# Bidirectional RWKV beside neighbourhood attention: one scan for the decays, division at the attention's output, tails first in a round, both directions' sigmoids together

## The chip, the cores and the metric

One Trainium2 chip, one of its cores. The metric is the device time of one execution in microseconds, median of several runs.

## What is computed

A token sequence of 512 with 1024 channels goes through a first block of two layers (mixer, cross attention, convolutional FFN) and then a second block: RWKV7 in both directions, neighbourhood attention, sigmoid gates, an output projection and 32 routed experts. The change touches RWKV and attention, which in the reference read

```python
def rwkv_log_decay(lora, w0, up):
    w_raw = (w0 + jnp.tanh(lora) @ up).astype(jnp.float32)
    return -jnp.exp(-jax.nn.softplus(-w_raw) - 0.5)
def rwkv_step(S, inp):
    r_t, w_t, k_t, v_t, kk_t, a_t = inp
    sa = jnp.einsum('dbhij,dbhj->dbhi', S, -kk_t)
    S = (S * w_t[..., None, :] + sa[..., :, None] * (kk_t * a_t)[..., None, :]
         + v_t[..., :, None] * k_t[..., None, :])
    y = jnp.einsum('dbhij,dbhj->dbhi', S, r_t)
    return S, y
...
        s = jnp.where(col_mask[:, None, :], s, NEG_INF)
        prob = jax.nn.softmax(s, axis=(-2, -1))
        return jnp.einsum('bhqrk,bhrkd->bhqd', prob, v_blk)
```

The log of a decay is thus −e^−0.5 times a sigmoid. There are 8 RWKV heads of 64 channels and 8 attention heads of 64; the attention's window is 8 rows of 16 columns of a 64-column grid, and all 512 keys are scored with a bias that masks the rest.

## The kernel before

Everything is float32. Large projections stream their weights in units of 128x2048 numbers; ACT makes a high part (L552, `act_split`), DVE the low part (L556, `dve_split`), and PE multiplies three times (L569). Seven PSUM banks rotate: `take_bank` (L513) makes PE wait until the last reader of that bank has marked it. All waits are semaphore waits in an engine's own in-order queue.

RWKV is computed by **quarters** t = 0 to 3, each of 128 channels (two heads), in both directions d = 0, 1, over 8 chunks of 64 tokens. Each engine has a generator for each part: `quarter(t)` holds a key part (L2280, L2543, L2710) and two `direction(t, d)` parts (PE L2298, ACT L2556, DVE L2722, POOL L2913). A direction runs as follows.

- Preparation, PREP_STEPS = 8 steps: PE multiplies the low-rank inputs for decay and `a` (tile `rw_lora_w`; d picks the row half), ACT takes sigmoids (L2566, L2568), DVE scales the first by −e^−0.5 (`ts`, L596), scans it per chunk with a reset mask (L2737), and forms `before` = cumulative − own (L2747) and `rest` = total − cumulative (L2754; L2756 and L2757 for d = 1). ACT takes exponentials of these (DC, R, A, B at L2581–L2584, H at L2586), DVE multiplies them onto r, kk, k (L2750, L2762, L593, L2767, L2768), POOL multiplies H onto K and B for the token side (L2930, L2932).
- 22 steps: PE forms the chunks' products, a triangular inverse in six levels (products of `rw_X`, `rw_XT`, `rw_U`; ACT copies U at L2610; DVE masked copies L2800, L2803), the UW products (`rw_GA,rw_XT`, ACT copy L2626), four banks of MN products (`rw_TB,rw_UW`; DVE L2812, L2814, L2817) and seven steps of the state, each a PE product `rw_S,rw_MT` and a DVE add L2831.
- `tail(t)`, 5 steps: normalisation of y, bonus and gate.

**Attention** has 8 units u (four head pairs, two halves of the queries). A unit has four score tiles of 128x512: PE scores, DVE adds the bias and takes the maximum (L2880), ACT exponentiates with row sums (L2671), DVE takes the reciprocal of the sum (L2889) and multiplies the whole tile by it (L596), PE transposes sixteen 128x128 pieces (L2506), ACT copies them (L2680), PE multiplies with v, ACT copies the output 128x256 (L2688).

What orders all this is `side_by_side` (L2032): in each round every engine advances the running quarters' parts (key, d = 0, d = 1), then the tails, then, in four of five rounds, attention. A new quarter begins every NEXT_AT = 16 rounds, so its preparation lies beside the last rounds of the quarter before; the first one's lies beside the gate projections (`beside_gate`, L2028). All engines walk through the same rounds. SP issues the stores of finished parts (`y_spill`) and loads of weight units in the same order of rounds.

## Time and profile before

| | us |
|---|---|
| median of three runs (lowest, highest) | 2575.53 (2573.32, 2575.6) |
| profiled execution, its span | 2572.24, 2570.9 |
| PE busy | 2450.4 |
| DVE busy | 1390.5 |
| ACT busy | 943.4 |
| POOL busy | 244.0 |
| granted clock, mean over the span | 0.984 |

The profiled execution is a single one; its parts are read as times from the span's start. Busy times of different engines overlap. The granted clock is a share of TensorE's full speed.

### The profile page before, as it was taken

The page shows a single profiled execution, that of the slowest core. Times are in us where ns is not written, and L with a number is a line of the kernel's source. Part 1 is how long each engine was busy: PE and PEld are TensorE (multiplying, and loading weights), DVE is VectorE, ACT ScalarE, POOL GpSimd, SP SyncE. Part 2 cuts the span into 40 slices and gives each one's busy share as a digit, 9 for nine tenths or more (in the row PEclk, how much of TensorE's full clock was granted, in tenths as well). Part 3 has the DMA queues.
Part 4 walks back from the last instruction along what each step waited for, and adds up shares of the span by engine and source line. Part 5 has one row for each costly group of instructions (what it writes and reads, how often), then busy time and mean ns, then how long its engine had stood idle before and what let it go on. Part 6 is the DMA issues. An engine that isn't in the chain of part 4 may idle for free.

```text
span 2570.9 us, 40805 instructions
## 1 busy us (share of the span) xinstructions
PE 2450.4 (95%) x17416; PEld 1842.1 (72%) x17416; DVE 1390.5 (54%) x1951; ACT 943.4 (37%) x1276; POOL 244.0 (9%) x204
## 2 busy tenths in 40 slices
PE   8998999999999989999999999999888889899996
PEld 6777878888887658878888887877776677633332
DVE  6776446454556866446454557574567755511112
ACT  4454333232333244233232344334646643411111
POOL 1002010000000101010000020000011102133331
PEclk9999999999999999999999999999999999999998
DMA  4223222222223423222222224433312123499994
GB/s 184 88 77 120 102 82 99 98 93 104 83 99 117 141 89 115 99 82 99 98 96 100 83 98 151 176 123 128 82 34 44 40 97 131 186 373 380 380 398 169
DMA packets 100562, 343.18 MB, mean 133 GB/s; under 512 B 41376, under 2 KB 49952, under 8 KB 66592
## 3 DMA queue, kind: packets, MB, share of 16 engines
q1 hardware_dynamic: 86560, 332.15, 35.8%
q0 software_dynamic: 13824, 8.44, 1.1%
q8 instruction: 139, 2.28, 0.4%
q14 instruction: 39, 0.32, 0.0%
HBM read 368.31 MB, written 30.93 MB: 155 GB/s over the span
## 4 chain that ended last, share of the span: by engine, by line
PE 83%; DVE 8%; ACT 4%; DMA 2%; issue 2%; SPq 1%; POOL 0%; DVEq 0%; ACTq 0%; POOLq 0%
PE bank L569 81%; DVE w_lo L556 1%; PE bank L3178 1%; ACT w_hi L552 1%; DMA w_raw<-stream 1%; DVE square L1975 1%; ACT rw_LT L2600 0%; PE bank L2506 0%; DMA e_w_raw<-y_rows 0%; PE bank L3200 0%; SPq L1581 0%; DVE na_score L2880 0%; DMA x<-x_spill 0%; DMA xa_mem<-mem_in 0%; PE bank L2375 0%
## 5 line engine op out<-in xcount | busy, mean ns | idle before, releaser
L569 PE MATMUL bank<-xg_hi,w_hi 128*128 128x512 f32 x1568 | 618.5, 398 | 11.9 <-DVE xg_lo L593 11.9
L569 PE MATMUL bank<-xg_hi,w_lo 128*128 128x512 f32 x1536 | 598.8, 390 | 0.0
L569 PE MATMUL bank<-xg_lo,w_hi 128*128 128x512 f32 x1504 | 586.0, 390 | 0.0
L556 DVE TENSOR_TENSOR w_lo<-w_raw,w_hi 128x2048 fp32r<-128x2048 f32 x165 | 380.8, 2309 | 199.1 <-ACT w_hi L552 198.7
L552 ACT ACTIVATE w_hi<-w_raw 128x2048 fp32r<-128x2048 f32 x165 | 314.5, 1906 | 246.4 <-PE bank L569 208.6
L569 PEld LDWEIGHTS bank<-xg_hi,w_hi 128*128 128x128 f32 x1568 | 294.5, 188 | 83.5 <-DVE w_lo L556 11.9
L569 PEld LDWEIGHTS bank<-xg_hi,w_lo 128*128 128x128 f32 x1536 | 288.8, 188 | 60.8
L569 PEld LDWEIGHTS bank<-xg_lo,w_hi 128*128 128x128 f32 x1504 | 282.8, 188 | 62.7 <-issue 4.8
L569 PE MATMUL bank<-f_h_hi,w_hi 128*128 128x512 f32 x384 | 151.3, 394 | 0.0
L569 PE MATMUL bank<-f_h_hi,w_lo 128*128 128x512 f32 x384 | 150.5, 392 | 0.0
L569 PE MATMUL bank<-f_h_lo,w_hi 128*128 128x512 f32 x384 | 149.0, 388 | 0.0
L569 PE MATMUL bank<-e_over_ring,e_h_turned 128*64 128x512 f32 x560 | 124.4, 595 | 0.0
L758 DVE TENSOR_TENSOR x<-bank,x 128x512 f32<-128x512 f32 x80 | 55.0, 687 | 118.0 <-PE bank L569 118.0
L3477 DVE TENSOR_TENSOR e_he<-e_he,bank 128x256 f32<-128x256 f32 x24 | 10.1, 421 | 171.1 <-ACT e_he L3298 171.1
L593 DVE SCALAR_TENSOR_TENSOR f_g<-f_z,vec_sb,f_g 128x510 f32<-128x510 f32 x96 | 72.0, 751 | 44.2 <-ACT f_g L1512 42.5
L1512 ACT ACTIVATE f_g<-f_z,vec_sb 128x512 f32<-128x512 f32 x48 | 39.2, 816 | 150.5 <-DVE f_z L1537 150.5
L569 PEld LDWEIGHTS bank<-e_over_ring,e_h_turned 128*64 128x64 f32 x560 | 38.7, 137 | 73.1 <-issue 73.1
L569 PEld LDWEIGHTS bank<-f_h_hi,w_lo 128*128 128x128 f32 x384 | 72.1, 188 | 16.9
L569 PEld LDWEIGHTS bank<-f_h_lo,w_hi 128*128 128x128 f32 x384 | 72.1, 188 | 16.1
L569 PEld LDWEIGHTS bank<-f_h_hi,w_hi 128*128 128x128 f32 x384 | 72.2, 188 | 14.4
L632 ACT ACTIVATE xg_hi<-x,vec_sb 128x512 fp32r<-128x512 f32 x48 | 34.7, 724 | 120.2 <-DVE x L758 98.3
L667 POOL TENSOR_TENSOR square_sum<-square 128x512 f32<-128x512 f32 x7 | 10.7, 1523 | 704.1 <-ACT square L638 686.5
(501 smaller groups left out, 4138.1 us busy)
## 6 DMA issues: line engine op xcount, KB each, us to landing
w_raw<-stream SPq DMA_DIRECT2D x165, 1024.0 KB, 4.8
e_over_ring<-expert_rows SPq DMA_DIRECT2D x70, 1024.0 KB, 10.6
e_w_raw<-expert_rows SPq DMA_DIRECT2D x26, 1024.0 KB, 9.9
p_spill<-p_stage SPq DMA_DIRECT2D x36, 256.0 KB, 2.1
na_bias<-bias_na SPq DMA_DIRECT2D x32, 160.0 KB, 4.2
mix_gate<-p_spill SPq DMA_DIRECT2D x16, 256.0 KB, 5.3
...
```

What stands on the lines that cost most here:

```text
L552: A.activation(ring(m)["hi"][m % SLOTS][:, :], ring(m)["raw"][m % RAW][:, :], ACT.Copy).then_inc(*w_hi.mark(m))
L556: V.tensor_tensor(ring(m)["lo"][m % SLOTS][:, :], ring(m)["raw"][m % RAW][:, :], ring(m)["hi"][m % SLOTS][:, :].bitcast(F32), ALU.subtract ...
L569: return T.matmul(out_ap, lhsT, rhs, start=first, stop=last, skip_group_check=True)
L593: return V.scalar_tensor_tensor(out=out_ap, in0=in0, scalar=scalar, in1=in1, op0=op0, op1=op1)
L632: A.activation(xg_of(i)[0][:, j, :], x[:, j, :], ACT.Identity, scale=vcol(NORMS[i], j)).then_inc(*act_norm.mark(i, "hi", j))
L667: G.tensor_tensor(square_sum_of(i), square[:, 0, :], square[:, 1, :], ALU.add).then_inc(*pool_norm.mark(i, "sum", 1))
L758: V.tensor_tensor(x[:, j, :], held(*tag, j)[:, :], x[:, j, :], ALU.add).then_inc(*added.mark(*tag, j))
L1512: A.activation(m["g"][:, s, :], m["z"][:, s, :], ACT.Identity, scale=f_tap(l, ch)(CONV_F - 1), bias=vcol(f"f_dw_b{l}", ch)).then_inc(*act_ ...
L1975: V.reciprocal(square[:, c, :], root[:, :]).then_inc(*dve_p.mark("qk_inv", t, c))
L3178: mm = T.transpose(b[:, c * P:(c + 1) * P], e_h_row[:, k % ROWS_AHEAD, kt * P:(kt + 1) * P], const("ident"))
L3477: V.tensor_tensor(e_he[:, k % 2, :], e_he[:, k % 2, :], held("e_gate", k)[:, D_EXPERT:], ALU.mult).then_inc(*dve_e.mark("he", k))
```

## The change

1. **Decays.** The sigmoids are scanned as they are, in rows of 8x65 with a leading zero in every chunk, so that the 520 results hold both the inclusive sums (columns 1 to 64) and the exclusive ones (0 to 63). The factor −e^−0.5 moves into the scale of ACT's exponentials. The scaling, `before` and, for d = 0, `rest` are not computed; d = 1 has one subtraction of 520 columns, one step earlier. The H exponentials go, and POOL multiplies K and B by the chunk's whole decay (DC) instead.
2. **Attention.** The exponentials are transposed as they are. One reciprocal 128x4 per unit; PE spreads the four rows of 1/sum over 64 partitions into the free half of the output's bank (four matmuls, ahead of the product with v), and DVE multiplies ACT's copy of the output by it. The bank is free only after this multiplication. The store of the output and its first use in the mixing wait for DVE.
3. **Tails** come first in each round, and a tail's first step directly behind its quarter's last.
4. **Sigmoids**: d = 1's low-rank matmuls and sigmoids move to the same step as those of d = 0.

The diff, with the context cut; left out are two lines in which a store and the mixing wait for `dve_na` instead of `act_na`.

```diff
@@ -122,6 +122,9 @@
+SUMS = CHUNK + 1
+
+
 def _window():
@@ -151,7 +154,7 @@
     c["strict1"], c["incl1"] = t < s, t <= s
-    c["reset"] = np.broadcast_to(np.arange(S) % CHUNK != 0, (P, S))
+    c["reset"] = np.broadcast_to(np.arange(8 * SUMS) % SUMS != 0, (P, 8 * SUMS))
     return {k: np.ascontiguousarray(v, np.float32) for k, v in c.items()}
@@ -2003,6 +2006,9 @@
                     *dve_kk.mark("omka"))
+                V.wait_ge(*dve_kk.at("masks"))
+                for d in range(2):
+                    V.memset(by_sums(rw_lw[d])[:, :, 0], 0.0).then_inc(*dve_kk.mark("before", d))
                 V.wait_ge(*dve_kk.now())
@@ -2035,12 +2041,13 @@
                 begun += 1
+            advance(others)
             for t, parts in list(running):
...
                     others.append(tail(t))
-            advance(others)
+                    advance(others[-1:])
             if step * 8 % 10 < 8:
@@ -2097,13 +2104,18 @@
+    def by_sums(ap):
+        return ap.rearrange("p (c t) -> p c t", t=SUMS)
+
     def even_odd(ap):
...
     rw_masks_f32 = x[:, 3:5, :].rearrange("p a b -> p (a b)")[:, 0:2 * LEVELS * HEAD]
-    rw_temps = [[x[:, 3, :], x[:, 4, :], x[:, 5, :], x[:, 6, :]],
-                [x[:, 7, :], square[:, 0, :], square[:, 1, :], root[:, :]]]
-    kk_root, kk_inv, tail_root, tail_inv = [rw_key[:, 1, 8 * i:8 * i + 8] for i in range(4)]
+    temp_x = x[:, 3:8, :].rearrange("p a b -> p (a b)")
+    rw_lw, rw_sums = [[temp_x[:, 8 * SUMS * i:8 * SUMS * (i + 1)] for i in of] for of in ((0, 3), (1, 2))]
+    rw_rest = by_sums(rw_key[:, :, :].rearrange("p a b -> p (a b)")[:, 0:8 * SUMS])
+    DECAY = -float(np.exp(-0.5))
+    kk_root, kk_inv, tail_root, tail_inv = [rw_key[:, 1, 64 + 8 * i:72 + 8 * i] for i in range(4)]
     wl, al, gl = x[:, 0, :], x[:, 1, :], x[:, 2, :]
@@ -2301,12 +2313,12 @@
             XT = one["XT2"][:, t % 2]
-            yield from steps(1 + d)
+            yield from steps(1)
             for m, (name, low) in enumerate((("lw", wl), ("a", al))):
...
                     *done.mark(name, t))
-            yield from steps(PREP_STEPS - 1 - d)
+            yield from steps(PREP_STEPS - 1)
             b = take_bank(T, ("At", t, d), by_act, "At", t, 1)
@@ -2502,13 +2514,18 @@
                         if k == 0:
-                            T.wait_ge(*dve_na.at("p", u, i))
+                            T.wait_ge(*act_na.at("e", u, i))
                         mm = T.transpose(b[:, i * P:(i + 1) * P], na_score[:, i, k * P:(k + 1) * P], const("ident"))
...
                 yield
-                b = take_bank(T, ("na_o", u), act_na, "out", u)
+                b = take_bank(T, ("na_o", u), dve_na, "out", u)
+                T.wait_ge(*dve_na.at("inv", u))
+                for i in na_order:
+                    at = 2 * P + P * (i % 2)
+                    matmul(T, b[half_rows(i // 2), at:at + P], na_stat[:, i, 2:3].to_broadcast([P, HEAD]),
+                           const("ident"))
                 if half == 0:
@@ -2556,34 +2573,32 @@
             one = rw[d]
-            yield from steps(1 + d)
-            t0, t1, t2, t3 = rw_temps[d]
+            yield from steps(1)
+            t0, t1, sums = by_sums(rw_lw[d])[:, :, 1:SUMS], square[:, d, :], by_sums(rw_sums[d])
             w0, a0 = (("w0_f", "a0_f"), ("w0_b", "a0_b"))[d]
-            dR, dA, dH = (t2, t3, t0) if d == 0 else (t1, t0, t3)
+            dR, dA = (sums[:, :, 1:SUMS], sums[:, :, 0:CHUNK]) if d == 0 else (rw_rest[:, :, 0:CHUNK], rw_rest[:, :, 1:SUMS])
             A.wait_ge(*by_pe.at("lw", t))
             if t:
-                A.wait_ge(*pool_rw[d].at("tokB", t - 1))
-            A.activation(t0, held("lw", t, d)[:, :], ACT.Sigmoid, bias=vcol(w0, t)).then_inc(*done.mark("lw", t))
+                A.wait_ge(*by_dve.at("kka", t - 1))
+            A.activation(t0, by_chunk(held("lw", t, d)[:, :]), ACT.Sigmoid, bias=vcol(w0, t)).then_inc(*done.mark("lw", t))
             A.wait_ge(*by_pe.at("a", t))
             A.activation(t1, held("a", t, d)[:, :], ACT.Sigmoid, bias=vcol(a0, t)).then_inc(*done.mark("a", t))
-            yield from steps(3)
+            yield from steps(3 + d)
             if t:
...
             yield
-            A.wait_ge(*by_dve.at("cumulative", t))
-            A.wait_ge(*by_dve.at("rest", t))
+            A.wait_ge(*by_dve.at("cumulative" if d == 0 else "rest", t))
             if t:
...
                 A.wait_ge(*by_pe.at("y", t - 2))
-            A.activation(one["DC"][:, :], by_chunk(t2)[:, :, CHUNK - 1], ACT.Exp).then_inc(*done.mark("DC", t))
-            A.activation(r_of(d, t), dR, ACT.Exp).then_inc(*done.mark("R", t))
-            A.activation(a_of(d), dA, ACT.Exp).then_inc(*done.mark("A", t))
-            A.activation(one["B"][:, :], dR, ACT.Exp, scale=-1.0).then_inc(*done.mark("B", t))
+            A.activation(one["DC"][:, :], sums[:, :, CHUNK], ACT.Exp, scale=DECAY).then_inc(*done.mark("DC", t))
+            A.activation(by_chunk(r_of(d, t)), dR, ACT.Exp, scale=DECAY).then_inc(*done.mark("R", t))
+            A.activation(by_chunk(a_of(d)), dA, ACT.Exp, scale=DECAY).then_inc(*done.mark("A", t))
+            A.activation(by_chunk(one["B"][:, :]), dR, ACT.Exp, scale=-DECAY).then_inc(*done.mark("B", t))
             yield
-            A.activation(dH, dH, ACT.Exp).then_inc(*done.mark("H", t))
             yield from steps(PREP_STEPS - 6 - d)
@@ -2728,13 +2743,14 @@
             XT = one["XT2"][:, t % 2]
-            t0, t1, t2, t3 = rw_temps[d]
+            t0, t1, sums = rw_lw[d], square[:, d, :], by_sums(rw_sums[d])
             up, low = up_low[d]
...
             V.wait_ge(*by_act.at("lw", t))
-            ts(V, t0, t0, -float(np.exp(-0.5)), None, ALU.mult).then_inc(*done.mark("lw", t))
-            V.wait_ge(*done.now())
-            V.tensor_tensor_scan(t2, rconst("reset"), t0, 0.0, ALU.mult, ALU.add).then_inc(*done.mark("cumulative", t))
+            if t:
+                V.wait_ge(*by_act.at("B", t - 1))
+            V.tensor_tensor_scan(rw_sums[d], rconst("reset"), t0, 0.0, ALU.mult, ALU.add).then_inc(
+                *done.mark("cumulative", t))
             yield
@@ -2743,18 +2759,13 @@
             V.tensor_tensor(Kh, Kh, k_, ALU.mult).then_inc(*done.mark("kd", t))
-            V.wait_ge(*done.at("cumulative", t))
-            V.tensor_tensor(t3, t2, t0, ALU.subtract).then_inc(*done.mark("before", t))
+            if d == 1:
+                V.wait_ge(*done.at("cumulative", t))
+                V.tensor_tensor(rw_rest, sums[:, :, CHUNK:SUMS].to_broadcast([P, 8, SUMS]), sums, ALU.subtract).then_inc(
+                    *done.mark("rest", t))
             yield
...
             V.tensor_tensor(Bh, kk, t1, ALU.mult).then_inc(*done.mark("kka", t))
-            total = by_chunk(t2)[:, :, CHUNK - 1:CHUNK].to_broadcast([P, 8, CHUNK])
-            V.wait_ge(*done.now())
-            if d == 0:
-                V.tensor_tensor(by_chunk(t0), total, by_chunk(t2), ALU.subtract).then_inc(*done.mark("rest", t))
-            else:
-                V.tensor_tensor(by_chunk(t0), total, by_chunk(t2), ALU.subtract).then_inc(*done.mark("rest0", t))
-                V.tensor_tensor(by_chunk(t1), total, by_chunk(t3), ALU.subtract).then_inc(*done.mark("rest", t))
             yield
@@ -2865,6 +2876,11 @@
+        def normalised(u):
+            out = na_out[:, 2 * P * (u % 2):2 * P * (u % 2 + 1)]
+            V.wait_ge(*act_na.at("out", u))
+            V.tensor_tensor(out, out, held("na_o", u)[:, 2 * P:4 * P], ALU.mult).then_inc(*dve_na.mark("out", u))
+
         def attention():
@@ -2883,16 +2899,15 @@
                         yield
+                yield
                 for i in na_order:
-                    st = na_stat[:, i, 0:4]
                     V.wait_ge(*act_na.at("e", u, i))
-                    V.reciprocal(st[:, 2:3], st[:, 1:2]).then_inc(*dve_na.mark("inv", u, i))
-                    V.wait_ge(*dve_na.now())
-                    ts(V, na_score[:, i, :], na_score[:, i, :], st[:, 2:3], None, ALU.mult).then_inc(
-                        *dve_na.mark("p", u, i))
+                if u:
+                    V.wait_ge(*pe_na.at("out", u - 1))
+                V.reciprocal(na_stat[:, :, 2], na_stat[:, :, 1]).then_inc(*dve_na.mark("inv", u))
                 yield
                 yield
-                yield
+                normalised(u)
@@ -2914,7 +2929,7 @@
             Bh, Kh, ksum = one["Bh"][:, :], one["Kh"][:, :], rw_ksum[:, t % 2, :]
-            dH = rw_temps[d][0 if d == 0 else 3]
+            whole = one["DC"][:, :].unsqueeze(2).to_broadcast([P, 8, CHUNK])
             yield from steps(PREP_STEPS)
@@ -2923,13 +2938,13 @@
             yield
-            G.wait_ge(*by_act.at("H", t))
+            G.wait_ge(*by_act.at("DC", t))
             G.wait_ge(*by_dve.at("K", t))
...
                 G.wait_ge(*pool_rw[1].at("ksum", t))
-            G.tensor_tensor(Kh, Kh, dH, ALU.mult).then_inc(*done.mark("tokK", t))
+            G.tensor_tensor(by_chunk(Kh), by_chunk(one["K"][:, :]), whole, ALU.mult).then_inc(*done.mark("tokK", t))
             G.wait_ge(*by_dve.at("B", t))
-            G.tensor_tensor(Bh, Bh, dH, ALU.mult).then_inc(*done.mark("tokB", t))
+            G.tensor_tensor(by_chunk(Bh), by_chunk(one["B"][:, :]), whole, ALU.mult).then_inc(*done.mark("tokB", t))
             yield
```

DVE around the last level's masked copies of XT at the third quarter's boundary (L2803 becomes L2814; `rw_kk`, `rw_Kh`, `rw_Bh` are the next quarter's preparation, L2812 and L2823 the MN products' readers). Before:

```order
L2803 COPY_PREDICATED rw_XT<-rw_level_masks,bank 128x512 x2
L2719 TENSOR_TENSOR rw_kk<-rw_kk,bank 128x512
L596 TENSOR_SCALAR rw_Kh<-x,vec_sb,rw_omka 128x512
L2745 TENSOR_TENSOR rw_Kh<-rw_Kh,rw_rkv 128x512
L2747 TENSOR_TENSOR x<-x 128x512
L596 TENSOR_SCALAR x<-x 128x512
L2737 SCALAR_TENSOR_TENSOR square<-rw_constants,x 128x512
L2750 TENSOR_TENSOR rw_Bh<-rw_kk,x 128x512
L2754 TENSOR_TENSOR x<-x 128x512
L596 TENSOR_SCALAR rw_Kh<-square,vec_sb,rw_omka 128x512
L2745 TENSOR_TENSOR rw_Kh<-rw_Kh,rw_rkv 128x512
L2747 TENSOR_TENSOR root<-square,x 128x512
```

After:

```order
L2752 SCALAR_TENSOR_TENSOR x<-rw_constants,x 128x520
L2814 COPY_PREDICATED rw_XT<-rw_level_masks,bank 128x512 x2
L2734 TENSOR_TENSOR rw_kk<-rw_kk,bank 128x512
L599 TENSOR_SCALAR rw_Kh<-square,vec_sb,rw_omka 128x512
L2761 TENSOR_TENSOR rw_Kh<-rw_Kh,rw_rkv 128x512
L2752 SCALAR_TENSOR_TENSOR x<-rw_constants,x 128x520
L2907 RECIPROCAL na_stat<-na_stat 128x4
L2768 TENSOR_TENSOR rw_Bh<-rw_kk,square 128x512
L599 TENSOR_SCALAR rw_Kh<-square,vec_sb,rw_omka 128x512
L2761 TENSOR_TENSOR rw_Kh<-rw_Kh,rw_rkv 128x512
L2764 TENSOR_TENSOR rw_key<-x 128x520
```

Eleven instructions stood between the masked copies and the first L2812, which comes next, and nine stand before the first L2823, one of them a reciprocal; the scan of d = 0 now lies ahead of the copies.

DVE at the start of the state steps at the same boundary (L2831 becomes L2842). Before:

```order
L593 SCALAR_TENSOR_TENSOR rw_AR<-rw_AR,rw_kk 128x512
L2750 TENSOR_TENSOR rw_Bh<-rw_kk,square 128x512
L2756 TENSOR_TENSOR x<-square 128x512
L2757 TENSOR_TENSOR square<-square,root 128x512
L2831 TENSOR_TENSOR rw_S<-bank,rw_N 128x64 x2
L2767 TENSOR_TENSOR rw_K<-rw_B,rw_Kh 128x512
L2768 TENSOR_TENSOR rw_B<-rw_B,rw_Bh 128x512
L2762 TENSOR_TENSOR rw_AR<-rw_AR,rw_rkv 128x512
L593 SCALAR_TENSOR_TENSOR rw_AR<-rw_AR,rw_kk 128x512
L2831 TENSOR_TENSOR rw_S<-bank,rw_N 128x64 x2
```

After:

```order
L596 SCALAR_TENSOR_TENSOR rw_AR<-rw_AR,rw_kk 128x512
L2768 TENSOR_TENSOR rw_Bh<-rw_kk,square 128x512
L2842 TENSOR_TENSOR rw_S<-bank,rw_N 128x64 x2
L2778 TENSOR_TENSOR rw_K<-rw_B,rw_Kh 128x512
L2779 TENSOR_TENSOR rw_B<-rw_B,rw_Bh 128x512
L2773 TENSOR_TENSOR rw_AR<-rw_AR,rw_rkv 128x512
L596 SCALAR_TENSOR_TENSOR rw_AR<-rw_AR,rw_kk 128x512
L2882 TENSOR_TENSOR na_out<-na_out,bank 128x256
L2842 TENSOR_TENSOR rw_S<-bank,rw_N 128x64 x2
```

Two subtractions are gone from in front of the first adds, and the attention's multiplication L2882 stands before the second.

ACT at the third quarter's boundary, from the sigmoids on. Before:

```order
L2566 ACT_TABLE_LOAD
L2566 ACTIVATE x<-bank,vec_sb 128x512
L2568 ACTIVATE x<-bank,vec_sb 128x512
L2671 ACT_TABLE_LOAD
L2671 ACTIVATE na_score,na_stat<-na_score,na_stat 128x512 x2
L2610 ACTIVATE rw_U<-bank 128x512 x2
L2566 ACT_TABLE_LOAD
L2566 ACTIVATE x<-bank,vec_sb 128x512
L2568 ACTIVATE square<-bank,vec_sb 128x512
L2680 ACTIVATE na_pT<-bank 128x512 x2
L2626 ACTIVATE rw_UW<-bank 128x512 x4
```

After:

```order
L2583 ACT_TABLE_LOAD
L2583 ACTIVATE x<-bank,vec_sb 128x8x64
L2585 ACTIVATE square<-bank,vec_sb 128x512
L2583 ACTIVATE x<-bank,vec_sb 128x8x64
L2585 ACTIVATE square<-bank,vec_sb 128x512
L2686 ACT_TABLE_LOAD
L2686 ACTIVATE na_score,na_stat<-na_score,na_stat 128x512 x2
L2625 ACTIVATE rw_U<-bank 128x512 x2
```

The four sigmoids stand in one piece before the exponentials and the copies of U, behind one table load.

## Rows read from the trace of the kernel before

**Rows 1.** The page: its head, and part 4, the chain that ended last by engine.
```profile
span 2570.9 us, 40805 instructions
...
PE 83%; DVE 8%; ACT 4%; DMA 2%; issue 2%; SPq 1%; POOL 0%; DVEq 0%; ACTq 0%; POOLq 0%
```

**Rows 2.** Windows: stretch, us, busy (x instructions) PE, PEld, DVE, ACT, POOL, PEclk, DMA share, GB/s.
```profile
1812.00:2150.00 338.00, 297.86 (x7191) 240.66 (x7183) 217.10 (x534) 180.61 (x335) 32.63 (x26) 0.97 0.22 59
...
1864.00:1868.00 4.00, 3.48 (x58) 2.96 (x62) 3.79 (x8) 2.39 (x6) 0.00 (x0) 0.60 0.03 8
```

**Rows 3.** PE's timeline, 1857 to 1880: start, us, engine, line, op, out<-in, xcount, [idle before <-releaser].
```profile
1857.22 1.09 PE L569 MATMUL bank<-const_sb,rw_key 128*64 128x128 f32 x16
1858.25 3.71 PE L569 MATMUL bank<-rw_GA,rw_XT 64*64 64x128 f32 x64
1863.16 0.30 PE L2506 MATMUL bank<-const_sb,na_score 128*128 128x128 f32 x1 [1.20 <-DVE na_stat L2889]
...
1864.84 1.33 PE L2506 MATMUL bank<-const_sb,na_score 128*128 128x128 f32 x5 [0.27 <-DVE na_score L596]
...
1871.38 0.45 PE L569 MATMUL bank<-rw_TB,rw_UW 64*64 64x128 f32 x8 [1.34 <-DVE rw_S L2821]
...
1876.03 1.09 PE L2506 MATMUL bank<-const_sb,na_score 128*128 128x128 f32 x8
1878.97 0.37 PE L569 MATMUL bank<-rw_S,rw_MT 64*64 64x64 f32 x2 [1.84 <-DVE rw_S L2831]
```

**Rows 4.** Groups of instructions of DVE by form, 1740 to 2160: busy, mean ns | idle before.
```profile
L596 DVE TENSOR_SCALAR na_score<-na_score,na_stat 128x512 f32<-128x512 f32 x32 | 15.5, 486 | 1.1
...
L2812 DVE TENSOR_TENSOR rw_MT<-rw_MT,bank 128x256 f32<-128x256 f32 x16 | 6.6, 414 | 9.2 <-PE bank L569 9.2
...
L2889 DVE RECIPROCAL na_stat<-na_stat 128x1 f32<-128x1 f32 x32 | 4.9, 154 | 0.0
...
L596 DVE TENSOR_SCALAR x<-x 128x512 f32<-128x512 f32 x8 | 3.2, 404 | 0.9 <-ACT x L2566 0.9
...
L2756 DVE TENSOR_TENSOR x<-square 128x512 f32<-128x512 f32 x4 | 2.8, 691 | 0.1
...
L2747 DVE TENSOR_TENSOR x<-x 128x512 f32<-128x512 f32 x4 | 2.7, 684 | 0.0
```

**Rows 5.** DVE's timeline at the second quarter's boundary.
```profile
1878.01 0.68 DVE L2757 TENSOR_TENSOR square<-square,root 128x512 f32<-128x512 f32 x1
1878.61 0.34 DVE L2831 TENSOR_TENSOR rw_S<-bank,rw_N 128x64 f32<-128x64 f32 x2
```

**Rows 6.** PE's timeline, gaps at the later boundaries.
```profile
1952.51 0.45 PE L569 MATMUL bank<-rw_TB,rw_UW 64*64 64x128 f32 x8 [2.94 <-DVE rw_AR L2817]
...
2034.11 0.45 PE L569 MATMUL bank<-rw_TB,rw_UW 64*64 64x128 f32 x8 [1.67 <-DVE rw_AR L2817]
...
2041.70 0.27 PE L569 MATMUL bank<-rw_S,rw_MT 64*64 64x64 f32 x2 [1.31 <-DVE rw_S L2831]
...
2094.41 2.37 PE L569 MATMUL bank<-rw_X,rw_LT 64*64 64x64 f32 x64 [0.58 <-DVE rw_XT L2803]
```

**Rows 7.** Timelines at the stage's end: ACT's weight split, and PE's longest pause.
```profile
2106.11 1.91 ACT L552 ACTIVATE w_hi<-w_raw 128x2048 fp32r<-128x2048 f32 x1 [0.96 <-DMA w_raw<-stream]
...
2117.37 0.37 PE L569 MATMUL bank<-rw_TB,rw_UW 64*64 64x64 f32 x2 [2.73 <-issue]
```

**Rows 8.** PE's timeline, the low-rank products of the third quarter.
```profile
1931.28 1.55 PE L569 MATMUL bank<-x,rw_lora_w 64*128 64x512 f32 x3
...
1936.07 3.04 PE L569 MATMUL bank<-x,rw_lora_w 64*128 64x512 f32 x6
```

**Rows 9.** ACT's timeline: a table load and the sigmoid behind it.
```profile
1854.76 1.28 ACT L2566 ACT_TABLE_LOAD   x1
1856.06 0.69 ACT L2566 ACTIVATE x<-bank,vec_sb 128x512 f32<-128x512 f32 x1
```

**Rows 10.** Groups of ACT by form, 1740 to 2160: the copy of the attention's output.
```profile
L2688 ACT ACTIVATE na_out<-bank 128x256 f32<-128x256 f32 x8 | 3.0, 379 | 14.4 <-PE bank L569 14.4
```

4 lines of the change are left out of this document (2 added, 2 removed).

## The prediction

> **What bounds the kernel now.** I read the page first: the chain that ended last lies on PE for 83% of the span, DVE 8%, ACT 4% [rows 1]. The change touches the stage where RWKV quarters and attention run side by side, so I then read the windows: in 1812–2150 PE is busy for 297.86 of 338 us, DVE for 217.10 and ACT for 180.61 [rows 2]. DVE and ACT have slack on the mean, and PE can gain at most the 40.1 us in which it idles, plus what the clock loses behind the idle stretches. Those lie mainly where one quarter ends and the next is prepared: in PE's timeline of the second quarter's boundary the reader sees transposes that wait for DVE's normalisation, then products that wait for a copy of S, then an S step that waits 1.84 us for DVE [rows 3]. So a removed DVE or ACT instruction counts only where it stands ahead of what such a gap waits for. I go from gap to gap, and write sums against the profiled execution, 2572.24 us; the median of the runs, 2575.53, lies 3.29 us above it. A change in time moves both alike.
>
> **What goes from DVE.** From its groups [rows 4]: 32 normalisations of 0.486 and 32 reciprocals of 0.154 make 20.5 us; eight scalings of 0.404 are 3.2; eight subtractions L2747 of 0.684 are 5.5; of twelve subtractions like L2756 (0.691) four remain, which is 5.5. That removes 34.7 us. It adds eight multiplications 128x256, priced by L2812 at 0.414, and eight reciprocals of 0.154 or little more: 4.6. Net 30 us of DVE's 217, nearly all of it beside a busy PE and worth nothing there. What remains, boundary by boundary:
>
> **Second quarter's boundary (1856–1880).** The UW products end at 1858.25+3.71 = 1861.96 and the transposes behind them at 1864.84+1.33 = 1866.17, which is 4.2 us; eight back to back take 1.09 [rows 3]. They wait for the pairs of reciprocal and normalisation, which stand behind preparation work on DVE. Afterwards they wait for ACT's exponentials, which end before the UW products: 3.1, of which I take **3.0**. The later gap of 1.84 us before an S step ends with the adds at 1878.61, and these stand right behind L2756 and L2757 [rows 5]. Both go from this place, two pitches of about 0.6: **1.2**.
>
> **Third and fourth boundaries, and the end.** The gap of 2.94 before the MN products waits for DVE, whose queue held the preparation. The order above shows it shorter by L2747 twice, a scaling and L2754, longer by the 520-wide subtraction: 0.68+0.40+0.69 = 1.8, less overlap of about 0.07 each. The same gap is 1.34 at 1871.38, where nothing stood in the way [rows 3, 6], a floor for the hop. So 2.94 shrinks to about 1.4: **1.5**. At 2034.11 the gap is 1.67 and falls to the floor: **0.3**. At 2041.70 it is 1.31, of which I leave the price of one new multiplication standing in front: **0.8**. The gap 0.58 at 2094.41 waits for a masked copy behind normalisations: **0.6** [rows 6]. At the end ACT waits 0.96 for a weight unit whose transfer SP issues behind the store of a tail's result. With the tail a step earlier those 0.96 us go at best; DVE's multiplication waits for an output copy that ACT makes behind this weight split, at 0.37–0.75. I take **0.2** [rows 7].
>
> **Lora products.** Two matmuls of opposite row halves overlap: the first group at 1931.28 contains them and begins with a pair, while the six records at 1936.07 (three matmuls, two row halves) follow singly at 1.01 each, 3.04 for three [rows 8]. With both directions together, a pair costs about one and a half of a single one. Near the gate projections and at the fourth boundary: **1.0** and **0.6**.
>
> **Costs.** (a) PE gets four matmuls per unit that spread 1/sum. The nearest row is a product with the same constant as moving side, eight instructions in 1.09 us [rows 3], so four are about 0.52 and eight units 4.1. They could cost nothing if each fell into a gap. About a quarter of that should fall into gaps that stay open, since such stand at three boundaries and eight units spread over them: **3.1**; bounds 0 and 4.1. (b) ACT does four sigmoids in one piece ahead of the last level's copies of U, two more than before at 0.69 each less some overlap [rows 9]. At the second and third boundaries this delays the XT products by 0 to about 1.2; between them PE has lora or attention work for half of it: **1.3** for both. (c) The eight H exponentials vanish from ACT, and six of 58 table loads; ACT is not the bound, POOL's multiplication keeps its size and starts earlier: 0. (d) The scan of 520 columns instead of 512 adds 1.5% of 1.2 us eight times, hidden under PE: 0. (e) Two memsets per run: 0. (f) The bank of an attention output is held until DVE's multiplication, ACT's copy (0.379, [rows 10]) plus 0.414 longer. Seven banks rotate, so 0 in my sum; it returns as a rival.
>
> Gains 3.0+1.2+1.5+0.3+0.8+0.6+0.2+1.6 = 9.2; costs 4.4; net 4.8.
>
> **The clock.** In 1864–1868, behind the idle of the transposes, PE was granted 0.60 (a mixture of 1.2 and 2.4 GHz) while 3.48 of 4 us were busy [rows 2]: at full clock that work takes 2.1. If the transposes run back to back, this stretch keeps its clock: up to 1.4, and I take all of it but nothing elsewhere: **1.5** with rounding. Forecast: 6.3 us less, 2572.24−6.3 = 2565.9 for such an execution, and 2575.53−6.3 = 2569.2 for the median.
>
> **Table loads, weighed.** A load takes 1.28 us (1854.76) and the next ACTIVATE starts at 1856.06, 1.30 after the load's start [rows 9]. At the second boundary two fewer loads stand ahead of ACT's later work. The Trainium skill, "ScalarE: Activation LUTs", section "What ACT_TABLE_LOAD costs", puts a further drain of 1380 ns behind each switch, 2.66 in all. No such drain is between these two rows. By the page six fewer loads would free 16 us of ACT instead of 7.7, and with a load on the path at each boundary the sum would be some 2.8 us better; by the row it stays as it is, and I follow the row.
>
> **Rivals.**
> *Gains that return as the next wait.* All queues are in order, and a gap closed on PE may open at its next wait: PE's chain runs through ACT and DVE hops that keep their 1.3 us. Then half of the first three gains stays (2.9), with the lora overlap 1.6, against spreading at its full 4.1 and the sigmoids' 1.3, no clock regained: 0.9 slower, 2576.4. For it: pauses of PE with no releaser, 2.73 at 2117.37 [rows 7], may also land elsewhere. Against it: the 4.2 us of the transposes are a plain wait with a named cause.
>
> *Slower: the multiplication blocks DVE.* At each of eight units DVE must wait for PE's spreading and PV and for ACT's copy, before it gets to the masked copies or S adds behind. If PE then waits on those, a hop of 1.3 [rows 6] and 0.414 come per unit: 1.7×8 = 13.7. With costs (a) and (b) in full 5.4 and gains 9.2 this is +9.9, 2585.4. It decides as soon as more than five of the eight units are caught, where the sum passes +5. Against it: the multiplication stands four rounds behind the reciprocal, and PV had ended before; in the S scan's order above it stands ahead of the adds, so one or two units are caught, not eight.
>
> *More clock.* If fewer gaps keep the clock high at every boundary, the loss in the stage comes back too: 0.03 of 298 busy us is 9 us [rows 2], of which 8.5 minus my 1.5 could go. That gives 2575.5−13.5 = 2562, a few us around it. The Trainium skill, "TensorE: Matmul & The Clock Gate", section "Part 1: The HAM clock gate (the "warmup" mystery)", says that activity releases the throttle and idleness brings it back, so that shorter gaps pay more than their length. The trace agrees as to direction (0.60 behind idle). But gaps of 1.3 us remain at every boundary, so I give it little.
>
> **How the numbers follow.** A difference under 0.2% (5.15 us) can't be told from no change; faster means below 2570.4, slower above 2580.7. Chances: forecast 0.48, its own range 2565 to 2573 (unknown sizes: spreading 0 to 4.1, XT delay 0 to 2.4, clock 0 to 1.5), three quarters of it below 2570.4; returning waits 0.29; blocked DVE 0.11; more clock 0.12. Faster 0.36+0.12+0.02 = 0.50, same 0.12+0.26 = 0.38, slower 0.11+0.01 = 0.12. The range runs from 2560 (most of the more-clock case) to 2579 (all of the returning waits); it leaves out the blocked DVE and a tail of the more-clock case.
>
> **What would show it.** Right: transposes of the second quarter's boundary in 1.1 us directly behind UW, no gap there; no L2756/L2757 before the S adds and a gap of about 0.7 for 1.84; MN gap near 1.4 at the third; spreading at 0.5 us per four matmuls; DVE's busy time in the stage 30 us lower and PE's some 3 us higher; clock above 0.9 behind the transposes; 52 loads. Wrong: spreading above 0.6 per unit, PE gaps released by the new DVE multiplication or by na_out, XT products of the last level waiting over 1 us for ACT, or a stage as long as before though the named gaps are gone.

## The result, and the profile after

The changed kernel takes 2558.3 us (median of four, 2554.23 to 2558.95) against 2574.43 for the kernel before: ratio 0.9936, 95% interval 0.9922 to 0.995, so 16.5 us less. A second series gave 0.9936 again (0.9923 to 0.995). The forecast was 6.3 us less with a range down to 2560: the sign was right, but the kernel gained 2.6 times as much.

Two executions of the changed kernel were profiled, 2554.23 and 2556.24 us; the one of before is 2572.24. Windows of the stage, columns as in [rows 2], first the changed kernel's first profile (the stage ends 17 us earlier there, so its window ends at 2133 and not at 2150):

```profile
1812.00:2133.00 321.00, 287.10 (x7264) 234.50 (x7256) 193.40 (x469) 171.69 (x326) 29.82 (x26) 0.99 0.23 62
...
1864.00:1868.00 4.00, 2.76 (x132) 2.65 (x125) 2.15 (x7) 4.00 (x10) 0.00 (x0) 1.00 0.02 4
...
2096.00:2100.00 4.00, 3.41 (x108) 3.44 (x110) 1.84 (x6) 1.73 (x1) 0.00 (x0) 0.59 0.67 260
```

The second:

```profile
1810.00:2133.00 323.00, 290.29 (x7249) 237.78 (x7242) 192.07 (x466) 170.38 (x324) 29.78 (x26) 0.98 0.23 62
...
1856.00:1860.00 4.00, 4.00 (x59) 3.66 (x58) 2.09 (x4) 0.38 (x1) 0.00 (x0) 0.71 0.78 126
1934.00:1938.00 4.00, 4.00 (x74) 3.73 (x72) 1.46 (x2) 0.00 (x0) 0.00 (x0) 0.65 1.25 193
```

In these windows DVE is busy 24 us less (27.0 over the whole run, 1390.5 to 1363.5), where 30 were forecast, and PE is busy 10.8 us less, where some 3 more were forecast. The table loads are 52, as forecast. The clock drops in one place of the first profile and in four of the second; before it dropped in six. PE's waits by releaser in the stage (us in total, times, longest); before, 1806 to 2146:

```profile
PE bank L569 <- DVE rw_TB L2785: 8.9, 8, 1.6
PE bank L569 <- issue: 8.5, 7, 2.7
PE bank L569 <- DVE rw_AR L2817: 7.1, 3, 2.9
PE bank L569 <- DVE rw_S L2831: 4.6, 4, 1.8
...
PE bank L569 <- ACT rw_U L2610: 1.2, 1, 1.2
PE bank L2506 <- DVE na_stat L2889: 1.2, 1, 1.2
```

After, 1806 to 2129:

```profile
PE bank L572 <- DVE rw_TB L2796: 8.9, 8, 1.6
PE bank L572 <- DVE rw_AR L2828: 6.8, 4, 3.1
PE bank L572 <- ACT rw_U L2625: 5.9, 4, 2.4
PE bank L572 <- issue: 4.9, 4, 1.9
PE bank L572 <- DVE rw_S L2842: 3.0, 3, 1.3
```

The wait for the division (`na_stat L2889`) is gone, those for S have shrunk, and in their place stand waits for ACT's copies of U, 1.2 before and 5.9 now. (An "issue" wait, called a pause below, is idle time of PE that no instruction of another engine is seen to end.) Pauses that nothing releases ("issue") fell from 10.0 in all (8.5 here, 1.4 before transposes) to 5.5. In PE's timeline the places that the forecast named:

```profile
1758.22 1.99 PE L572 MATMUL bank<-x,rw_lora_w 64*128 64x512 f32 x8
...
1854.52 0.68 PE L572 MATMUL bank<-rw_XT,rw_U 64*64 64x64 f32 x16 [1.88 <-ACT rw_U L2625]
...
1857.56 3.71 PE L572 MATMUL bank<-rw_GA,rw_XT 64*64 64x128 f32 x64
1861.20 1.09 PE L2518 MATMUL bank<-const_sb,na_score 128*128 128x128 f32 x8
...
1872.70 0.27 PE L572 MATMUL bank<-rw_S,rw_MT 64*64 64x64 f32 x2 [0.52 <-DVE rw_S L2842]
1874.73 0.66 PE L572 MATMUL bank<-const_sb,na_stat 128*64 128x128 f32 x8
1875.21 1.90 PE L572 MATMUL bank<-na_pT,na_v 128*64 128x256 f32 x16
...
1932.94 2.08 PE L572 MATMUL bank<-rw_XT,rw_U 64*64 64x64 f32 x64 [2.38 <-ACT rw_U L2625]
1944.70 0.45 PE L572 MATMUL bank<-rw_TB,rw_UW 64*64 64x128 f32 x8 [1.25 <-DVE rw_AR L2828]
2019.72 0.45 PE L572 MATMUL bank<-rw_TB,rw_UW 64*64 64x128 f32 x8 [1.24 <-DVE rw_AR L2828]
...
2096.59 0.70 PE L572 MATMUL bank<-rw_TB,rw_UW 64*64 64x128 f32 x8 [3.10 <-DVE rw_AR L2828]
```

The transposes follow the UW products directly and take 1.09 us. Four low-rank products (eight records) take 1.99 us, which is what each pair took before:

```profile
1755.92 1.98 PE L569 MATMUL bank<-x,rw_lora_w 64*128 64x512 f32 x4
...
1763.50 1.98 PE L569 MATMUL bank<-x,rw_lora_w 64*128 64x512 f32 x4
```

The last gap of the stage is longer than before, when it was

```profile
2112.36 0.45 PE L569 MATMUL bank<-rw_TB,rw_UW 64*64 64x128 f32 x8 [2.52 <-DVE rw_AR L2817]
```

### The profile page after: what moved, and what is told of

Its sections match the earlier page's. It is cut to its first block, busy times and chain, and to the rows that moved or that the text cites. A ratio compares the mean times of both kernels' runs of the same rounds, so it can differ in the third digit from the quotient of the medians.

```text
span 2552.9 us, 40871 instructions
## 1 busy us (share of the span) xinstructions
PE 2435.7 (95%) x17480; PEld 1835.0 (72%) x17480; DVE 1363.5 (53%) x1881; ACT 930.1 (36%) x1262; POOL 240.1 (9%) x204
## 4 chain that ended last, share of the span: by engine, by line
PE 85%; DVE 6%; ACT 4%; DMA 2%; issue 2%; SPq 0%; POOL 0%; DVEq 0%; ACTq 0%; POOLq 0%
PE bank L572 82%; DVE w_lo L559 1%; PE bank L3193 1%; DMA w_raw<-stream 1%; ACT w_hi L555 1%; DVE square L1978 1%; PE bank L2518 1%; ACT rw_LT L2615 0%; DMA e_w_raw<-y_rows 0%; DVE na_score L2896 0%; PE bank L3215 0%; SPq L1584 0%; DMA xa_mem<-mem_in 0%; DMA x<-x_spill 0%; PE bank L1367 0%
## 5 line engine op out<-in xcount | busy, mean ns | idle before, releaser
L555 ACT ACTIVATE w_hi<-w_raw 128x2048 fp32r<-128x2048 f32 x165 | 314.5, 1906 | 243.9 <-PE bank L572 210.5
L572 PEld LDWEIGHTS bank<-f_h_hi,w_lo 128*128 128x128 f32 x384 | 72.1, 188 | 16.9
```

Source lines behind the costliest of these rows:

```text
L555: A.activation(ring(m)["hi"][m % SLOTS][:, :], ring(m)["raw"][m % RAW][:, :], ACT.Copy).then_inc(*w_hi.mark(m))
L572: return T.matmul(out_ap, lhsT, rhs, start=first, stop=last, skip_group_check=True)
```

## The experiments

All ratios are against the kernel before, timed on the same chip; a thousandth is 2.6 us. Intervals are ±0.001 to ±0.0015 (shown for each), some 3 to 4 us, so a single microsecond is not told apart. "Clock lost" is the sum over the stage, in steps of 2 us, of PE's busy time times one minus the granted clock: 9.2 us before, 1.3 and 6.3 in the two profiles of the changed kernel. "Named waits" is the sum of PE's waits with a releaser, from 1806 to the stage's last product with `rw_lora_w` (2146.34 before, 2128.99 after): 31.8 before, 29.9 and 29.8 after. The changed kernel's second profile and series are the run `a_again`. It was to tell whether the small loss to the clock belongs to the kernel (then 0.9936 again and 1 to 3 us lost) or to that one execution (then 0.994 to 0.995 and 5 to 9 lost). The time came out as the first, the loss (6.3) as the second, so one profile does not give a kernel's loss to the clock.

### Each part alone

Edits: the hunks of the diff that belong to one part, on the kernel before. `b_div` has the waits on `e` and `inv`, the spreading, `normalised` and the new reciprocal. `b_tail`:

```diff
+            advance(others)
             for t, parts in list(running):
...
-            advance(others)
+                    advance(others[-1:])
```

`b_sig` (PE and ACT; ACT's exponentials keep their round):

```diff
-            yield from steps(1 + d)
+            yield from steps(1)
...
-            yield from steps(3)
+            yield from steps(3 + d)
```

`b_scan` is the rest: 520-column scans, DECAY in ACT's scale, no H.

> The kernel before with only the division at the attention's output. Theory A (short idle stretches cost mainly by the clock that falls behind them): the transposes' 3 us of waiting at the second quarter's boundary and the clock's dip behind them go, spreading costs 8 x 0.48 = 3.8 us: 3 to 5 us faster than before. Theory B (the pauses of PE without a releaser, 10.0 us before and 5.5 after, carry the rest and fall anew with any edit): the named wait 3 us against spreading 3.8, so within 1 us of before, except for what the pauses sum to. Theory C (waits alone, no clock): 1 us slower to 1 us faster, the clock's dips as many as before.

Measured 0.9989 (0.998 to 0.9999): 2.8 us faster. In its profile the transposes no longer wait, yet the last gap has grown to twice its size, because DVE's multiplication waits for an ACT copy behind a weight split, and DVE's own split stands behind it:

```profile
2113.16 0.70 PE L569 MATMUL bank<-rw_TB,rw_UW 64*64 64x128 f32 x8 [5.05 <-DVE rw_AR L2822]
```

The named waits are 31.2 us there, so all but 0.6 of what the transposes gave is lost again at the end; the pauses are 3 less (6.9), 9.0 us are lost to the clock. In this profile the gain is not the clock's; the pauses are its size, as theory B had it, but two profiles of one program can differ by more than this (1.0 in pauses, 5 in the clock), so it is not shown.

> The kernel before with only the tails first in each round. Theory A: the weight unit at the stage's end comes earlier, the 2.5 us gap there shrinks, nothing elsewhere: 0 to 2 us faster, dips of the clock as before but for the last. Theory B: pauses move, up to 3 us either way with no named wait changed. Theory C: 0 to 1 us faster.

Measured 0.9994 (0.9985 to 1.0003): 1.5 us faster, not told from nothing. Named waits 30.6 us, pauses 8.2.

> The kernel before with only both directions' low-rank products and sigmoids in one step. Pairs of products overlap (1.6 us less), but PE waits for ACT's copies of U at the second and third boundaries as in the changed kernel (1.88 and 2.38 us there). Theory A: 1 to 5 us slower, since new idle is added and the clock may fall behind it. Theory C: 2 to 3 us slower. Theory B: anything within 3 us of before.

Measured 0.9982 (0.9973 to 0.9992): 4.6 us faster, where A and C said slower and B within 3. The waits for U are as forecast (1.88 and 2.52, with the 1.22 that stood there before 5.6 us in all), but the low-rank products' busy time falls much further. Groups of PE by form, 1740 to the stage's end, first before, then `b_sig`:

```profile
L569 PE MATMUL bank<-x,rw_lora_w 64*128 64x512 f32 x32 | 15.8, 615 | 0.0
```
```profile
L569 PE MATMUL bank<-x,rw_lora_w 64*128 64x512 f32 x32 | 8.0, 615 | 0.0
```

Part of the 7.8 us had been shared with score products. Quarter by quarter, from the first low-rank product to the end of the score products beside them, the saving is 2.0, 1.6, 1.9 and 2.0: 7.5 us.

> The kernel before with only the one scan for the decays (factor in ACT's scale, no H exponentials). Theory A: the gaps of 1.84 and 2.94 us on PE shrink by 1.2 and 1.5 and the clock's dips behind them (1878 and 1952) go: 5 to 7 us faster. Theory C: 2 to 3 us faster, dips stay. Theory B: 2 to 3 us faster, with pauses unlike before.

Measured 0.9969 (0.9958 to 0.9981): 8.0 us faster, a little above A's 5 to 7, and by another road. The named waits fall by 7.0 us (31.8 to 24.8), the loss to the clock only by 1.9 (to 7.3), and the pauses hardly (9.8). The gap of 2.94 is gone, the one of 1.84 is 0.52, and the first transpose waits 0.15 instead of 1.20 [rows 3], since the scaling and a subtraction stood ahead of the normalisations too. A pause of 1.39 stands where the 2.94 was:

```profile
1863.19 0.30 PE L2517 MATMUL bank<-const_sb,na_score 128*128 128x128 f32 x1 [0.15 <-DVE na_stat L2894]
...
1950.37 0.21 PE L572 MATMUL bank<-rw_Lrk,rw_tok_V 64*64 64x64 f32 x1 [1.39 <-issue]
```

The four sum to 16.9 us, the whole gives 16.5; each carries some 2.6 us of noise.

### Each part taken away

The same hunks, reverted on the changed kernel.

> The changed kernel with attention normalised before the transposes, as before. Additive parts: it loses the 2.8 us that the division gave alone, 13.5 us faster than before remain. Interaction (the other parts already take the wait ahead of the transposes away, as the profile with the scan alone shows; spreading's 3.8 us and the wait at the stage's end are then pure cost): it loses nothing or wins 1 to 2 us, 16 to 18 us faster than before. Clock theory (every part is needed to keep the clock): it loses 5 us or more.

0.9948 (0.9935 to 0.9961), 13.4 us faster than before: the division is worth 3.1 in the whole, as alone. Additive holds.

> The changed kernel with the tails after the running quarters, as before. Additive: it loses 1.5 us, 15 us faster than before remain. Interaction (with the division alone the wait at the stage's end was 5.05 us, with tails first too it is 3.1): it loses 3 to 4 us, 12.5 to 13.5 faster than before. The wait ahead of the last MN products tells: 3.1 or about 5.

0.996 (0.9946 to 0.9973), 10.3 faster: it loses 6.2 us, four times what tails first gave alone. The last gap is 4.79 for 3.10, as the interaction said; that is 1.7 of the 6. Mean granted clock over its six runs 0.984, over the changed kernel's nine 0.986, which is the rest in size, but no wait is found that causes it, and with intervals of this width the 1.5 and the 6.2 are hardly told apart.

> The changed kernel with the decays as before (scaling, two scans, subtractions, H exponentials). Additive: it loses 8 us, 8.5 faster than before remain. Interaction with the division (some of DVE's relief is the same wait): it loses 5 to 6, 10.5 to 11.5 faster than before. Clock theory: it loses over 10 us.

0.9978 (0.9969 to 0.9987), 5.7 faster: it loses 10.8, more than the 8.0 that the scan gave alone, and in the range of the clock theory. Its profile has 34.8 us of named waits against 29.9, and 12.2 lost to the clock against 1.3 and 6.3; that the clock makes the difference rests on this one profile.

> The changed kernel with d = 1's low-rank products and sigmoids one step later, as before. Additive (what the fourth part gave alone): it loses 4.6 us, 12 us faster than before remain. By the traces: the overlap of row halves goes (7.5 us), the waits for U of 1.9 and 2.4 us go too: it loses 3 to 5. Interaction as for the other removals (each lost 1.3 to 3 us more than it gave alone): it loses 6 to 8.

0.9951 (0.9938 to 0.9965), 12.6 faster: it loses 3.9. Additive, and the waits for U of 1.88 and 2.38 are gone in its profile as they came (named waits 25.5).

### The low-rank products without the sigmoids

`a_lora`: ACT keeps `steps(1 + d)` and `steps(3)`, PE's products stay together.

> The changed kernel with d = 1's sigmoids (ACT) back where they were, one step later, and only PE's low-rank products of both directions in one step. Theory A (the fourth part wins by the overlap of opposite row halves, 15.8 to 8.0 us of PE in the profiles, and gives back 4.3 us in waits for ACT's copies of U, which stand behind four sigmoids): the overlap stays, the waits of 1.88 and 2.38 us go, 2 to 4 us faster than the changed kernel, so 18 to 21 us faster than before. Theory B (the sigmoids in one piece are what wins, by one table load instead of two in a boundary): 1 to 4 us slower than the changed kernel. Theory C (the banks held longer stall PE elsewhere): as the changed kernel.

0.9979 (0.9969 to 0.9989): 5.4 us faster than before, 11 slower than the changed kernel and 7 slower than `a_nosig`, which has neither. None of the three theories allowed for it. The overlap is there (8.0 us), and still it is much worse. The products fill banks that ACT reads only a round later, and the attention's scores and the XT products wait for these banks:

```profile
1854.36 1.37 PE L572 MATMUL bank<-na_qk 64*128 64x512 f32 x2 [3.21 <-ACT x L2583]
...
1936.51 3.30 PE L572 MATMUL bank<-rw_XT,rw_U 64*64 64x64 f32 x64 [3.80 <-ACT x L2583]
```

So A was wrong about the remedy: here the sigmoids, which free the banks, must go with the products. The waits for banks do not make up the 11 us, though: they stand in the place of those for U, and the named waits of this profile are 32.0 us, only 2.1 more than in the changed kernel, its pauses 6.3 and its loss to the clock 6.3. What the rest is stays open.

### ACT's order at the boundaries

`a_exps`: in ACT's `attention`, unit 1 gives its first pair of exponentials a round later and unit 3 its second pair, so that the copies of U come first. All else is the changed kernel.

```diff
+                if u == 1:
+                    yield
                 for i in na_order:
...
-                    if i // 2:
+                    if i // 2 and not (u == 1 and i == 2):
+                        yield
+                    if u == 3 and i == 2:
                         yield
-                yield
+                if u != 3:
+                    yield
```

> The changed kernel with the exponentials of the attention's second and fourth unit (their first pair in the one, their second in the other) behind ACT's copies of U at the second and third quarters' boundaries, not ahead of them. If ACT's order sets the waits of 1.88 and 2.38 us on PE: both fall below 0.7, 2.5 to 3.5 us faster than the changed kernel. If the transposes or the XT copies wait instead: as the changed kernel.

0.9907 (0.9892 to 0.9922), and again:

> The kernel of a_exps again, for its time and a second profile. It measured 22 us under before where the waits it takes away explain 4.3 and the changed kernel's 16.5 make 21. If that was the kernel: 0.990 to 0.992 again. If the luck of a few executions: 0.992 to 0.993, 18 to 20 us faster than before. The waits for U stay below 0.7 us either way.

0.9923 (0.9909 to 0.9936): some 20 to 24 us faster than before, 3 to 7 faster than the changed kernel. The repetition lies where the luck of a few executions was to put it, so the 3 is nearer than the 7; the waits taken away make 4.3. At the two boundaries PE no longer waits for U: the waits for it are 1.7 us in all where they were 5.9, and the named waits are 25.9 and 25.1. ACT's timeline of `a_exps` shows the copies directly behind the sigmoids, the table load and the exponentials after them:

```profile
1851.19 0.69 ACT L2583 ACTIVATE x<-bank,vec_sb 128x512 f32<-128x512 f32 x1
1851.76 0.70 ACT L2585 ACTIVATE square<-bank,vec_sb 128x512 f32<-128x512 f32 x1
1852.33 1.20 ACT L2625 ACTIVATE rw_U<-bank 128x512 f32<-128x512 f32 x2
1853.54 1.28 ACT L2688 ACT_TABLE_LOAD   x1
1854.84 0.72 ACT L2688 ACTIVATE na_score<-na_score,na_stat 128x512 f32<-128x512 f32 x1
```

### The last gap

`a_split` moves DVE's split of the mixing's first unit (2.28 us) from ahead of the readers of d = 0's MN products to behind them; `a_both` has it with `a_exps`.

> The changed kernel with DVE's split of the mixing's first weight unit (2.28 us) behind the copies of d = 0's MN products in the last quarter instead of ahead of them. If DVE's queue sets the last gap on PE (3.1 us): it falls to 1.2, 2 us faster than the changed kernel. If the weight split then is late for the mixing's matmuls, or the next wait takes the place: as the changed kernel.

0.9938 (0.9924 to 0.9951): as the changed kernel. The gap closed as forecast, and a pause opened 3 us behind it:

```profile
2101.09 0.45 PE L572 MATMUL bank<-rw_TB,rw_UW 64*64 64x128 f32 x8 [1.24 <-DVE rw_AR L2826]
...
2104.30 0.26 PE L572 MATMUL bank<-rw_UW,rw_TB 64*64 64x64 f32 x1 [2.21 <-issue]
```

> a_exps and a_split together: the exponentials behind the copies of U, and DVE's weight split behind the copies of d = 0's MN products. If the 1.9 us of the last gap on PE are real once nothing takes their place: 1 to 2 us faster than a_exps2. If a pause without a releaser follows the closed gap, as in a_split (2.21 us): the same as a_exps2.

0.9912 (0.9899 to 0.9926), against 0.9923 of `a_exps2` on the same chip: 2553.09 and 2554.23 us, inside the noise; its profile has a pause of 1.31 at this place. `a_both` and `a_exps` are the fastest versions here, both ahead of either kernel.

### The pauses

`b_nobias` and `a_nobias` leave out nine tenths of each bias load after the first unit's, so the later units work with stale bias:

```diff
-                            Y.dma_start(na_bias[a * HEAD:(a + 1) * HEAD, par, :, :],
+                            n = 1 if u else 10
+                            Y.dma_start(na_bias[a * HEAD:(a + 1) * HEAD, par, 0:n, :],
```

> The kernel before with the loads of the attention's bias cut to a tenth for all units but the first, so that the later units add stale bias (their output differs); the same number of transfers is issued. Theory D (PE's pauses without a releaser, 10 us of them in the stage, are its instructions held up behind these loads, since they follow some 7.5 us after each issue): the pauses near 1829, 1906, 1982 and 1986 go, the one at the stage's end (2.73, behind a weight load) stays, 5 to 8 us faster. Rival (the pauses come from PE's own queue and fall at fixed places of its program): the same time within 1 us, the pauses as before.

0.9982 (0.9973 to 0.9991): 4.6 us faster, and the pauses fall from 10.0 to 5.4. The one at 1829 is 1.09 for 1.92, those near 1906 and 1986 are gone, but the one behind 1980 stays:

```profile
1829.81 0.21 PE L569 MATMUL bank<-rw_U,rw_XT 64*64 64x64 f32 x1 [1.09 <-issue]
...
1981.37 1.35 PE L2507 MATMUL bank<-const_sb,na_score 128*128 128x128 f32 x8 [1.97 <-issue]
```

> The changed kernel with the same cut of the bias loads. Theory D: its pauses (4.5 to 5.5 us in two profiles, nearly all behind bias loads) go: 3 to 5 us faster than the changed kernel. If D holds and the changed kernel won 4 to 5 us of its 16 through shorter pauses, the two kernels without the loads lie 11 to 13 us apart instead of 16. Rival: as the changed kernel, 16 us faster than before.

0.9925 (0.9911 to 0.9938): 19.3 faster than before, 2.8 more than the changed kernel; its pauses are 3.9. So theory D is right for about half of the pauses of the kernel before: bias traffic lengthens them, and part remains without it. The time bears this out for the kernel before (4.6 us); for the changed kernel 2.8 us lie inside the noise. Without the loads the kernels lie 14.7 us apart, 1.8 less than with them, which the noise can't tell from none. How PE's instructions come to be late is not shown by any view, only that they are.

### The clock, and the price of spreading

`b_fill` adds, ahead of `b_n` for d = 1:

```diff
+            if d == 1:
+                for i in range(8):
+                    matmul(T, b_mz[0][:, 0:P], const("ident"), const("ident"))
```

> The kernel before with eight extra products of constants on PE (128x128 each, about 0.5 us in all at full clock) in the gap ahead of each quarter's second MN products, into a bank that is overwritten afterwards; nothing it computes changes. Clock theory (idle there lets the clock fall, and any activity keeps it): 1 to 3 us faster than before, mean granted clock 0.985 or more, fewer dips at the third and fourth boundaries and the end. Rival (the gap is set by DVE, the clock falls for other reasons): within 1 us of before, clock 0.984.

0.9996 (0.9987 to 1.0005): no difference; mean clock of its runs 0.984 against 0.983 before. The added products were longer than expected, 8.2 us of PE in all or 2.05 at each boundary instead of 0.5, and they stand where PE was waiting: the named waits are 24.0 us for 31.8. In its profile the drops at 1952 and 2056 are gone, but so is the one at 1864, where nothing was added, and one stands behind a pause of 1.99 at 1984.90, where before a like pause was followed by none; 6.4 us lost for 9.2. Whether filled gaps keep the clock up is thus not settled; filling them brings nothing that can be measured.

`a_spread2` has `for i in na_order + na_order` at the spreading.

> The changed kernel with the four products that spread 1/sum issued twice per unit; the result is the same. If they lie on PE's path at their traced pitch (0.48 us for four): 3.8 us slower than the changed kernel. If a part of them falls into gaps (my forecast took a quarter): 2.5 to 3 us slower. If they also hold DVE's multiplication up: over 4.

0.9938 (0.9924 to 0.9951): 0.5 us slower than the changed kernel, in an interval of 3. The profile shows the second four at their full pitch (0.44 us), so 3.5 us more of PE's path; it also shows no drop of the clock in the stage at all, and its five runs have the highest mean clock of all kernels here, 0.987. That extra products on PE's path cost less than their length in this stage is suggested, not shown: 3.5 us lie at the edge of the interval. That the clock pays the difference fits the numbers, but the profile of `a_both`, with no product added, shows no drop in the stage either.

## Why the prediction was wrong

By its own terms, with what they measured (profiles; us):

| term | forecast | measured |
|---|---|---|
| transposes behind UW | 3.0 | 3.2 |
| S step, 1.84 to 0.52 | 1.2 | 1.3 |
| MN gap, 2.94 to 1.25 | 1.5 | 1.7 |
| fourth boundary, 1.67 to 1.24 | 0.3 | 0.4 |
| S step at 2041.70, 1.31 to 0 | 0.8 | 1.3 |
| copy at 2094.41, 0.58 to 0 | 0.6 | 0.6 |
| low-rank products (forecast at two places, measured at four) | 1.6 | 7.5 |
| stage's last gap | 0.2 | −0.6 |
| XT waits for ACT's U | −1.3 | −4.3 |
| spreading | −3.1 | −3.9 |
| clock | 1.5 | 3.0 to 7.9 |
| pauses | 0 | 4.5 to 5.5 |

**The waits were read rightly.** Each gap of the trace that a removed DVE instruction stood ahead of shrank as worked out, to a floor of 1.24 to 1.25 rather than 1.34. One stretch was counted twice: the slow transposes after 1864 are in the 3.0 and again in the 1.5 for the clock, 0.6 us by their length (1.33 for five, 0.68 at the pitch of 1.09 for eight).

**The first failed step is the lora term**, "a pair costs about one and a half of a single one", counted at two places. I took a group of three records at 1931.28 for an overlapping pair, though it is two products of one direction, with score products beside; and the six at 1936.07, read as two row halves, are the two products of d = 1 and the gate's product over all 128 rows, which stands apart in `b_sig`. Four products of opposite row halves take 1.99 us, no more than two of one half, in all four quarters: 7.5 us of PE. At the two places that the forecast counted, this is 3.7 us in the changed kernel for its 1.6: 1.9 beside the gate projections, and 1.8 at the fourth boundary (6.79 us before and 4.99 after, from the first low-rank product to the score products).

**The second is the cover of the sigmoids' delay.** Their term was 1.3, and the waits for U grew by 4.3 at the second and third boundaries. ACT's part is the 1.2 of the forecast: from the first sigmoid to the first copy of U it took 4.00 us before and 5.16 after, and the table load and one pair of exponentials stand between in both kernels. First before, then the changed kernel, at the third boundary:

```profile
1933.93 0.69 ACT L2566 ACTIVATE x<-bank,vec_sb 128x512 f32<-128x512 f32 x1
...
1935.21 1.28 ACT L2671 ACT_TABLE_LOAD   x1
...
1937.93 1.06 ACT L2610 ACTIVATE rw_U<-bank 128x512 f32<-128x512 f32 x2
```
```profile
1927.15 0.69 ACT L2583 ACTIVATE x<-bank,vec_sb 128x512 f32<-128x512 f32 x1
...
1929.59 1.28 ACT L2686 ACT_TABLE_LOAD   x1
...
1932.31 1.05 ACT L2625 ACTIVATE rw_U<-bank 128x512 f32<-128x512 f32 x2
```

The rest is PE's. The forecast let "lora or attention work" cover half of the delay, and this change takes that work away: d = 1's products stood between the X and the XT products, where PE waits for U. Before, then after:

```profile
1934.05 2.08 PE L569 MATMUL bank<-rw_X,rw_LT 64*64 64x64 f32 x64
...
1939.03 2.08 PE L569 MATMUL bank<-rw_XT,rw_U 64*64 64x64 f32 x64
```
```profile
1928.48 2.08 PE L572 MATMUL bank<-rw_X,rw_LT 64*64 64x64 f32 x64
1932.94 2.08 PE L572 MATMUL bank<-rw_XT,rw_U 64*64 64x64 f32 x64 [2.38 <-ACT rw_U L2625]
```

So at these two boundaries the overlap gave nothing. From the first low-rank product to the XT products it was 7.55 and 7.75 us before and is 7.80 and 8.30 now, 0.8 us longer together; ACT sets this stretch. By this count the fourth part of the change is worth 3.7 less 0.8, or 2.9 us for the forecast's 0.3, and the runs have 4.6 alone and 3.9 taken away. `a_exps`, which puts the copies ahead of the load and the exponentials, takes the two waits away and wins 3 to 7 us.

**The third is what I held constant.** Pauses without a releaser were 10.0 us before. I treated them as noise that may land elsewhere. They go with the program: 10.0 and 10.3 in two profiles with the before's order (before, `b_fill`), 5.5, 4.5 and 4.8 in three with the changed one's (`a_spread2` the third), while the parts alone have 6.9 to 9.8. The bias loads lengthen them, as the runs without the loads show; which part of the change moved the two largest away is not shown, nor by what.

**The clock** was undersized. I gave back one of six drops. The first profile has one left, the second four; over nine runs the mean granted clock is 0.9857 against 0.984 before, and 0.0017 of 2574 is 4.4 us, an estimate. A single profile can't tell the size, since two of the same program differ by 4.9 us of lost clock at 2 us of time.

Against the second profile (16.0 us less) the parts are: pauses 5.5, named waits 2.1 (31.8 to 29.8), clock 3.0, low-rank products 7.5, less spreading 3.9, together 14.2; 1.8 is not assigned. Against the first (18.0 us less) the same sum gives 17.9, with 7.9 from the clock. That it closes so well is partly luck, since the time ahead of the stage varies too: in the stage itself, from 1808.25 (1808.42 and 1806.17 in the changed kernel's profiles) to the last product with `rw_lora_w`, the gain is 17.5 and 14.0 us and the parts without the first quarter's 1.9 make 16.0 and 12.2, so 1.5 and 1.8 stay unassigned. What was added up is the work and the waits of PE; only the four parts of the change, the order of ACT and the bias loads were tested by runs, the shares of clock and pauses were read from profiles.

The rival of more clock gave the nearest number (2562), but by luck: its mechanism carries about a quarter of the gain (4.4 of 16.5 by the mean clocks). The rival that blocks DVE reached PE at one unit only, the last: the multiplication started there after DVE had been idle for 7.54 us until ACT's copy (18.7 us before six of the eight units, which PE does not show elsewhere), where its order with the weight split costs 0.6 with tails first and 2.5 without.

On the table load the rows stand: in the changed kernel a load begins at 1851.18 and the next ACTIVATE at 1852.47, 1.29 us later. The Trainium skill, "ScalarE: Activation LUTs", section "What ACT_TABLE_LOAD costs", has a drain of about 1380 ns with each switch of tables; none appears here either, and the measurement decides.
